# Sums of blocks turned into additions and made by adding transfers; weights asked for from ScalarE's queue

## The reference, cut to what matters

```python
h = _rmsnorm(x, norm_w)
proj = jnp.einsum('bsd,df->bsf', h, w_in)
q_a, k_a, v_a, z_a, q_m, k_m, v_m, o_m, z_m, g = jnp.split(proj, offsets, axis=-1)
# group A: QK-norm, partial rotary, three (window, dilation) patterns mixed by softmax denominators
for window, dil in ((128, 1), (512, 4), (2048, 16)):
    o, lse = _dilated_band_attention(qa, ka, va, dil, window // (2 * dil))
attn = jnp.sum(mix_w[..., None] * jnp.stack(outs, axis=0), axis=0) * jax.nn.silu(z_a)
# group B: stabilised matrix memory, chunkwise, forward and backward, summed
hm = jax.nn.sigmoid(o_m) * _rmsnorm(h_fwd + h_bwd, m_norm_w) * jax.nn.silu(z_m)
y = jnp.concatenate([attn, hm], axis=-1)
out = x + jnp.einsum('bsf,fd->bsd', y, w_out)
```

## Time and profile before

| | before |
|---|---|
| median of three runs | 1996.13 us |
| the profiled execution | 1991.36 us |
| its span | 1989.6 us |
| PE busy | 1947.4 us, 98% |
| DVE busy | 1384.3 us, 70% |
| ACT busy | 889.3 us, 45% |
| POOL busy | 222.0 us, 11% |
| granted TensorE clock, mean | 0.997 |

### The profile page before, as it was taken

One profiled execution on the slowest core, in us unless ns is written; L12 is line 12 of the kernel. 1 busy time (PEld: TensorE's weight loads), 2 busy tenths in 40 slices (PEclk: granted clock), 3 DMA queues, 4 the chain that ended last, 5 costly groups with the idle time before them and its releaser, 6 DMA issues.

```text
span 1989.6 us, 27114 instructions
## 1 busy us (share of the span) xinstructions
PE 1947.4 (98%) x9089; PEld 1589.4 (80%) x9089; DVE 1384.3 (70%) x2791; ACT 889.3 (45%) x1422; POOL 222.0 (11%) x240
## 2 busy tenths in 40 slices
PE   8999999999999999999999999999999899999999
PEld 6888887888888888888887878787787677777787
DVE  7677868678768768767767575665666857667655
ACT  6554335344335435334453335545446463455222
POOL 0241000110110010010000111110110111111111
PEclk9999999999999999999999999999999899999999
DMA  6676543564564465365369864462655836347554
GB/s 210 218 272 229 190 160 113 139 151 126 134 162 119 108 159 148 107 159 148 115 206 369 208 154 92 116 175 50 169 121 131 263 75 191 99 119 209 104 117 106
DMA packets 159337, 310.37 MB, mean 156 GB/s; under 512 B 17072, under 2 KB 36048, under 8 KB 155488
## 3 DMA queue, kind: packets, MB, share of 16 engines
q1 hardware_dynamic: 128432, 247.81, 37.8%
q0 software_dynamic: 28608, 53.49, 17.3%
q10 hardware_dynamic: 2160, 7.34, 1.0%
HBM read 198.60 MB, written 118.37 MB: 159 GB/s over the span
## 4 chain that ended last, share of the span: by engine, by line
PE 84%; DMA 5%; DVE 5%; issue 4%; ACT 1%; SPq 0%; POOL 0%; DVEq 0%; ACTq 0%; POOLq 0%
PE ps L816 22%; PE ps L820 21%; PE ps L818 21%; PE ps L1019 3%; PE ps L988 2%; PE ps L1005 2%; DMA arena<-rot_dram 1%; PE ps L957 1%; PE ps L913 1%; PE ps L922 1%; PE ps L916 1%; PE ps L1023 1%; DMA rot_dram<-arena 1%; ACT w_hi L1056 1%; PE ps L1021 1%
## 5 line engine op out<-in xcount | busy, mean ns | idle before, releaser
L816 PE MATMUL ps<-t_hi,w_hi 128*128 128x512 f32 x2184 | 872.0, 399 | 24.4 <-issue 9.7
L820 PE MATMUL ps<-t_hi,w_lo 128*128 128x512 f32 x2184 | 853.5, 391 | 0.0
L818 PE MATMUL ps<-t_lo,w_hi 128*128 128x512 f32 x2184 | 853.2, 391 | 0.0
L816 PEld LDWEIGHTS ps<-t_hi,w_hi 128*128 128x128 f32 x2184 | 411.5, 188 | 125.3 <-issue 45.9
L820 PEld LDWEIGHTS ps<-t_hi,w_lo 128*128 128x128 f32 x2184 | 411.2, 188 | 87.7
L818 PEld LDWEIGHTS ps<-t_lo,w_hi 128*128 128x128 f32 x2184 | 412.1, 189 | 79.6
L1340 DVE TENSOR_TENSOR w_lo<-s_tmp,w_hi 128x512 fp32r<-128x512 f32 x312 | 221.5, 710 | 180.0 <-ACT w_hi L1056 169.2
L1056 ACT CAST w_hi<-s_tmp 128x512 fp32r<-128x512 f32 x312 | 193.9, 622 | 292.7 <-PE ps L820 273.2
L1340 DVE TENSOR_TENSOR w_lo<-w_raw,w_hi 128x512 fp32r<-128x512 f32 x234 | 165.4, 707 | 146.9 <-ACT w_hi L1056 140.6
L1056 ACT CAST w_hi<-w_raw 128x512 fp32r<-128x512 f32 x234 | 145.4, 621 | 225.4 <-PE ps L820 225.3
L413 POOL DMA_DIRECT2D fin_dram<-xt x32 | 28.1, 878 | 850.8 <-ACT xt L1069 829.7
(11 more groups left out here) (225 smaller groups left out, 2390.5 us busy)
## 6 DMA issues: line engine op xcount, KB each, us to landing
w_raw<-w_all_dram SPq DMA_DIRECT2D x320, 256.0 KB, 4.0
fin_dram<-xt SPq DMA_DIRECT2D x128, 256.0 KB, 4.3
fin_dram<-xt POOLq DMA_DIRECT2D x128, 256.0 KB, 5.0
arena<-fin_dram SPq DMA_DIRECT2D x64, 512.0 KB, 7.3
outT_dram<-xt POOLq DMA_DIRECT2D x60, 256.0 KB, 4.1
arena<-xT_dram SPq DMA_DIRECT2D x44, 256.0 KB, 6.0
arena<-xT_dram SPq DMA_DIRECT2D x16, 512.0 KB, 4.4
outT_dram<-xT_dram SPq DMA_DIRECT2D x16, 512.0 KB, 5.4
```

The costliest lines, as they stand in the source:

```text
L816: nc.tensor.matmul(ps[:, bank, :], hi, t_hi[:, n, k, :], start=new and k == 0, stop=False, skip_group_check=True)
L818: nc.tensor.matmul(ps[:, bank, :], hi, t_lo[:, n, k, :], start=False, stop=False, skip_group_check=True)
L820: mm = nc.tensor.matmul(ps[:, bank, :], lo, t_hi[:, n, k, :], start=False, stop=k == KP - 1, skip_group_check=True)
```

## The change

Four things change, and nothing of what is computed. The signs of the operands are chosen so that every sum of blocks, of x, y and weights, is an addition (one of the four weight sums excepted); for this the evictions of n = 1 and n = 3 become `scalar_tensor_tensor` (bank times -1, minus x1). The sums of y are then made by transfers that add in DRAM: SP copies or stores the first summand, POOL adds the second. For the mLSTM half this leaves DVE altogether and is spread over units 226 to 236 and 322 to 333; for the attention half heads 4 to 6 leave DVE. The splits of the exchanges get tables of their own (`HIGH_AT`, `LOW_AT`, `Y_HIGH`, `Y_LOW`). And the weights are asked for by ACT, as the last thing of its units n = 0 and n = 4.

```diff
-Y_SPLIT = {3: {3: 0, 5: 1, 6: 2, 8: 3, 9: 4, 10: 5, 11: 6}, 4: {3: 0, 5: 1, 6: 2, 7: 3, 8: 4, 9: 5, 10: 6}}
+HIGH_AT = {1: {1: 0, 2: 1, 4: 2, 6: 3, 7: 4, 9: 6, 10: 5}, 2: {1: 0, 4: 2, 8: 6}}
+LOW_AT = {1: {1: 0, 3: 1, 5: 2, 7: 3, 8: 4, 10: 6, 11: 5}, 2: {1: 0, 5: 2, 8: 6}}
+Y_HIGH = {3: {3: 0, 4: 1, 5: 2, 7: 3, 8: 4, 9: 5, 10: 6}, 4: {3: 0, 5: 1, 6: 2, 7: 3, 8: 4, 9: 5, 10: 6}}
+Y_LOW = {3: {3: 0, 5: 1, 6: 2, 8: 3, 9: 4, 10: 5, 11: 6}, 4: {3: 0, 5: 1, 6: 2, 7: 3, 8: 4, 9: 5, 10: 6}}
-YM_AT = 321
+YM_STEPS = (226, 231, 236, 322, 328, 333)
...
@@ sync: attention_loads
-                    sp.dma_start(y_sums[:, 0, :], y_dram[ATT_HEADS + h - KP][:, HALF:]).then_inc(ya_in, 16)
-                    sp.dma_start(y_sums[:, 1, :], ty_dram[1, SUMS.index(4)][:, h - KP, :]).then_inc(ya_in, 16)
...
+                if at == 22 and h < KP:
+                    sp.dma_start(ty_dram[1, SUMS.index(3), :, h, :], ystage[:, HALF:]).then_inc(ya_out, 16)
+                    sp.wait_ge(ya_sum, h + 1)
+                    sp.dma_start(ty_dram[1, 1:4, :, h, :].rearrange("i p s -> p i s"),
+                                 y_sums[:, 0, :].unsqueeze(1).to_broadcast([P, 3, HALF])).then_inc(ya_out, 16)
+
+            def ym_copies(u):
                 y = y_dram[0:ATT_HEADS].rearrange("k p s -> p k s")
+                if u == YM_STEPS[0]:
+                    sp.wait_ge(m_out, 16 * 2)
+                    for n in (4, 3):
+                        sp.dma_start(ty_dram[0, SUMS.index(n)], y[:, 0:KP, HALF:]).then_inc(ym_out, 16)
+                if u == YM_STEPS[2]:
+                    sp.wait_ge(ym_added, 16)
+                    sp.dma_start(ty_dram[0, SUMS.index(1)], ty_dram[0, SUMS.index(4)]).then_inc(ym_out, 16)
+                if u == YM_STEPS[4]:
+                    sp.wait_ge(ym_added, 48)
+                    sp.dma_start(ty_dram[0, SUMS.index(5)], ty_dram[0, SUMS.index(1)]).then_inc(ym_out, 16)
...
@@ sync: the loop over units
-                if g + 1 < NG:
-                    next_weights(g, n)
@@ scalar: build
-                n = {1: 0, 3: 2, 4: 1, 5: 3, 6: 4, 8: 6, 9: 5}.get(off)
-                if n is not None and not (b == 2 and n in KEPT):
+                n = HIGH_AT[b].get(off)
+                if n is not None:
                     t_high(b, n)
@@ scalar
+            def next_weights(g, n):
+                if n == 0:
+                    act.wait_ge(s_done, sums_before(g) + 3)
+                    load(g + 1, 1, 0, 0)
+                    act.wait_ge(lo_done, split_before(g - 1) + 6 if g > PLAIN else 4 * PLAIN)
+                    load(g + 1, 1, 1, 1 + (g + 1) % 2)
+                    act.wait_ge(lo_done, split_before(g) + 1)
+                    load(g + 1, 0, 0, 3)
+                if n == 4:
+                    act.wait_ge(lo_done, split_before(g) + 3)
+                    act.wait_ge(s_done, sums_before(g) + 4)
+                    load(g + 1, 0, 1, 4)
...
@@ vector: evict, n == 1 (n == 3 alike)
-                    nc.vector.tensor_tensor(x2, bank, x1, ALU.add).then_inc(ev_d, 1)
+                    nc.vector.scalar_tensor_tensor(x2, bank, -1.0, x1, ALU.mult, ALU.subtract).then_inc(ev_d, 1)
@@ vector: build_sums
-                if off in (4, 5):
-                    t_four(1, 2 * off - 8)
-                    t_four(1, 2 * off - 7)
+                if off in (6, 7, 8, 9):
+                    t_four(1, off - 6)
@@ vector: ym_sums taken out, ya_sums
+                if KP <= h < ATT_HEADS - 1:
+                    return
@@ gpsimd
+            def add_ym(u):
+                y = y_dram[0:ATT_HEADS].rearrange("k p s -> p k s")
+                if u == YM_STEPS[1]:
+                    pool.wait_ge(m_out, 16 * 2)
+                    pool.wait_ge(ym_out, 32)
+                    pool.dma_start(ty_dram[0, SUMS.index(4)], y[:, 0:KP, 0:HALF], accum_op=ALU.add).then_inc(ym_added, 16)
+                if u == YM_STEPS[3]:
+                    pool.wait_ge(m_out, 16 * M_HEADS)
+                    pool.wait_ge(ym_out, 48)
+                    for n in (1, 3):
+                        pool.dma_start(ty_dram[0, SUMS.index(n)], y[:, KP:, HALF:], accum_op=ALU.add).then_inc(ym_added, 16)
+                if u == YM_STEPS[5]:
+                    pool.wait_ge(ym_out, 64)
+                    pool.dma_start(ty_dram[0, SUMS.index(5)], y[:, KP:, 0:HALF], accum_op=ALU.add).then_inc(ym_added, 16)
+
+            def add_ya(h, at):
+                if KP <= h < ATT_HEADS - 1:
+                    if at == 22:
+                        pool.wait_ge(a_y, 4 * h + 4)
+                        pool.wait_ge(ya_out, 32 * KP)
+                        pool.dma_start(ty_dram[1, 0:3, :, h - KP, :].rearrange("i p s -> p i s"),
+                                       ystage[:, HALF:].unsqueeze(1).to_broadcast([P, 3, HALF]), accum_op=ALU.add
+                                       ).then_inc(ya_added, 16)
+                    if at == 24:
+                        pool.wait_ge(ya_added, 32 * (h - KP) + 16)
+                        pool.dma_start(ty_dram[1, SUMS.index(5), :, h - KP, :], ystage[:, 0:HALF], accum_op=ALU.add
+                                       ).then_inc(ya_added, 16)
```

More of the change, by code:

```diff
@@ L1243, in y_operands @@
                     act.dma_start(t_lo[:, off - 1].bitcast(F32), y_block(3, off - 1)).then_inc(t_in[off - 1], 16)
-                n = Y_SPLIT[b].get(off)
+                n = Y_HIGH[b].get(off)
                 if n is not None:
@@ L1256, in y_operands, with load @@
                         nc.scalar.copy(t_hi[:, n, KP - 1, :], last_head(n)).then_inc(th_done[n], 1)
+            def load(g, i, k, slot):
+                p, kh = GROUPS[g]
+                act.dma_start(w_raw[:, slot, :], w_all[(2 * p + i) * PIECES + 2 * kh + k]).then_inc(w_in[slot], 16)
+            def next_weights(g, n):
[6 more added lines that the diff above has]
+                    load(g + 1, 0, 0, 3)
+                if n == 4:
+                    act.wait_ge(lo_done, split_before(g) + 3)
+                    act.wait_ge(s_done, sums_before(g) + 4)
+                    load(g + 1, 0, 1, 4)
             def plain_hi(j):
@@ L1455, in build @@
                     build_sums(off)
-                n = {1: 0, 3: 2, 4: 1, 5: 3, 6: 4, 8: 6, 9: 5}.get(off)
-                if n is not None and not (b == 2 and n in KEPT):
+                n = LOW_AT[b].get(off)
+                if n is not None:
                     t_low(b, n)
@@ L1820, in ya_sums @@
                     dve.wait_ge(a_pv, 4 * h + 4)
-                    nc.vector.tensor_tensor(y_sums[:, 0, :], high, low, ALU.subtract).then_inc(ya_sum, 1)
+                    nc.vector.tensor_tensor(y_sums[:, 0, :], high, low, ALU.add).then_inc(ya_sum, 1)
                     return
-                dve.wait_ge(ya_in, 32 * (h - KP + 1))
-                nc.vector.tensor_tensor(y_sums[:, 1, :], high, y_sums[:, 1, :], ALU.subtract).then_inc(ya_sum, 1)
-                nc.vector.tensor_tensor(y_sums[:, 0, :], high, y_sums[:, 0, :], ALU.subtract).then_inc(ya_sum, 1)
+                dve.wait_ge(ya_in, 16)
+                nc.vector.tensor_tensor(y_sums[:, 1, :], high, y_sums[:, 1, :], ALU.add).then_inc(ya_sum, 1)
+                nc.vector.tensor_tensor(y_sums[:, 0, :], high, y_sums[:, 0, :], ALU.add).then_inc(ya_sum, 1)
                 dve.wait_ge(ya_sum, sums_of_y(h) + 1)
-                nc.vector.tensor_tensor(y_sums[:, 2, :], low, y_sums[:, 1, :], ALU.subtract).then_inc(ya_sum, 1)
+                nc.vector.tensor_tensor(y_sums[:, 2, :], low, y_sums[:, 1, :], ALU.add).then_inc(ya_sum, 1)
             def y_low(b, off):
-                n = Y_SPLIT[b].get(off)
+                n = Y_LOW[b].get(off)
                 if n is not None:
```

108 lines of the change are left out of this document (32 added, 76 removed).

## The result

| | before | after |
|---|---|---|
| median of the runs, four each | 1996.99 us | 2017.18 us (2011.86 to 2018.72) |
| ratio | | 1.0095, 95% interval 1.0069 to 1.0122 |
| profiled execution | 1991.36 us | 2016.79 us, span 2015.0 |
| granted clock, mean | 0.997 | 0.992 |

A forecast was written before the change was run, and what follows sets the result against it. PE, busy 98% of the span, was taken to bound the kernel, with little idle time to touch. Terms +0.6 - 2.2 + 1.8 - 0.4 - 2.8 - 1.6 + 1.0 + 1.0 + 0.2 = -2.4 us gave 1994 us, range 1984 to 2004.

The forecast's parts named there:

- The first exchange: First exchange: PE stands 4.7 us, mostly in one gap just ahead of product 5, against 4.1 now; +0.6 us.
- The mLSTM sums: Units' idle time at 1036 to 1060 us: DVE's sums for the mLSTM half go, -2.2 us, bounds 0 and -2.2.
- The second exchange's order: Second exchange: operand 2's low part moves from `off` 3 to 5; -0.4 us, bounds 0 and -1.5.
- The third exchange's gap: Third exchange: head 4's three sums leave DVE, so PE's gap of 4.56 us shrinks to about 2.8.
- The addition at unit 333: Unit 333, among the `t_dram` loads: a 1 MB addition replaces a 1 MB load; +1.8 us, bounds 0 and +3.6.
- Stores of heads 0 to 3: Heads 0 to 3: SP stores 1 MB instead of 256 KB while turned rows travel; +1.0 us, bounds 0 and +4.
- The additions of heads 4 to 6: POOL's queue: 768 KB additions ahead of turned rows' second store and loads; +1.0 us for three heads, bounds 0 and +8.
- gains of 1.6 and 2.8: DVE's sums gone: PE's gaps behind heads 5 and 6, -1.6 us; third exchange, gap and clock together, -2.8 us.
- rival B: POOL's additions hold up turned rows of heads 5 to 7 and the `t_dram` loads: +12 us, 2008 us; chance 0.12.
- a sign of being wrong: Trace after: landings of the 768 KB additions under 4 us or over 8 us would show the forecast wrong.
- The weights from ACT: Weights asked for by ACT: nearly all in time, 0, bounds 0 and +6; `w_raw` waits over 3 us would be wrong.
- The evictions: Evictions with a scalar: 0.05 us more each, 156 times, hidden by the products except in full stretches; +0.2 us.

The follow-up runs named there:

- e8: e3 with the mLSTM half's last copy and last addition moved from units 328 and 333 to 348 and 354: 1993.5 us, 0.9972 of the kernel before.
- e3: The changed kernel with the attention half's sums made by DVE and stored by SP as before, no addition in DRAM there: 2002.3 us, 1.0026.
- e9: e3 with SP's added 768 KB of stores in heads 0 to 3 put back, in unit 22 as in the change: 2012.6 us, 1.0071.
- e7: The changed kernel, additions of heads 4 to 6 taken from y_dram, behind the turned rows' loads (units 25 and 29, not 22 and 24): 2008.0 us, 1.0047.
- e1: The changed kernel with the weights asked for by SP again, as in the kernel before: 2020.2 us, 1.0119.
- e4: The changed kernel with the mLSTM half's sums made by DVE from loaded blocks as before: 2015.5 us, 1.0090.
- e10: The changed kernel, all parts kept, the sums' DRAM transfers moved to units where the queues are nearly idle: 1992.9 us, 0.9972 of the kernel before.

## Why the prediction was wrong, by its steps

**The first exchange** came as forecast: one gap just ahead of product 5, ended by the low part on DVE,

```profile
359.15 0.47 PE L799 MATMUL ps<-t_hi,w_hi 128*128 128x512 f32 x1 [2.94 <-DVE t_lo L1453]
```

and the whole exchange neither better nor worse (excess of 300 to 380: 9.2 us before and after). PE stands 4.6 us from 324 to 370, forecast 4.7, and 4.1 before. Counting DVE's work against 11 units of products was the right way to read it.

**The mLSTM sums**, -2.2 us: the window has no gap any more. Right. **The second exchange's order**, -0.4 us, is hidden by the next step.

**The third exchange's gap**, 4.56 to 2.8 us: it is 2.79 us. Right, but a gap of 7.6 us that the forecast did not have follows it.

**The addition at unit 333**, +1.8 us with bounds 0 and +3.6: this step failed. It priced the addition by bytes over a mean rate, 6.8 us for 1 MB, and took half of the difference to what went away. The place costs 11 us (e8 against e3, 0.54%, with the copy ahead of it). An addition of 1 MB took 14.5 us with no large transfer beside it and 19.7 us here; PE waits here for the landing of each load, one product at a time, the loads land 6 to 7 us later, and PE then loses clock too. The row with `t_dram` already at 1.0 us of wait said that there was no slack.

**Stores of heads 0 to 3**, +1.0 us with bounds 0 and +4: this step failed too, with 9 us measured (e9 against e3). The bytes, 0.13% or 2.6 us, lie within the bounds. The other 6 us are a step that the prediction did not have: SP's wait for DVE's sum, moved from unit 23 to 22, holds back the next head's first load, so that 768 KB, both loads of `rs_dram` and the second store of turned rows fall together.

**The additions of heads 4 to 6**, +1.0 us with bounds 0 and +8, against gains of 1.6 and 2.8, so -3.4 us together: in their place they cost 0.24%, 5 us (after against e9, the two intervals overlap), and in units 25 and 29 they give as much (e7 against e9). The mechanism was rival B's, priced at 12 us with a chance of 0.12, and the rows for it were there: a store and a load within 0.6 us in one queue, a wait of DVE for them. The forecast set it aside because "DVE has slack before PE stands". At the third exchange DVE had none. The prediction charged heads 5 to 7 and did not look at which exchange head 5's turned rows fall in. The 768 KB were priced at 5.0 us; they landed in 9.5, 11.2 and 18.1 us, over the 8 us that it had named as a sign of being wrong. Even so rival B falls short of the measured time by 9 us: its sum had the last addition at 3.6 us and the stores of heads 0 to 3 not at all.

**The weights from ACT**, 0 with bounds 0 and +6: four pairs lie between -0.25% and +0.19%, 5 us to either side, so no constant cost, but no constant zero either. The waits of DVE and ACT for `w_raw` beside the kernel's first grow to 3.4 + 1.8 + 0.4 = 5.6 us, over the 3 us named as a sign; with the weights on SP (e1) 3.7 us of such waits stay and the time is no better. **The evictions**, +0.2 us for 0.05 us more each: the two forms take the same time at this shape (L1358 and L1361 685 ns, L1354 and L1357 691 and 690 ns as the median of 78), so there was nothing to charge.

Along the chain of kernels from before to after, the sum is -0.28% for the rest of the change (e8), +0.54% for the late copy and addition (e3), +0.45% for the stores (e9) and +0.24% for the additions of heads 4 to 6. These are differences of neighbours, so they add up to the 0.95% whatever they hold; each has an error of 0.2 to 0.3%, and taking a part out of the changed kernel instead gives other sizes (0.48% for the additions in e7, 0.05% for the whole mLSTM half in e4). Against the forecast's terms the first two steps are 9 and 8 us too small, and the third, 5 us of cost for 3.4 us of gain, is 8 us off.

## What to carry to other kernels

A transfer is priced by what lands beside it and what stands behind it in its queue and behind its wait in its engine's program, not by its bytes over a mean rate: the same parts of a change made this kernel 20 us slower or 6 us faster (e10), by the unit in which their transfers were asked for. When work is taken off a busy engine and put into DRAM, look first for the stretches with a low DMA share, and put it there, behind the small transfers for which an engine is waiting. Where a trace shows even 1 us of wait for a load, that load has no slack left, and what is put beside it must be priced by what it does to the landing. And one pair of kernels is not enough for a gain of a few us: here the same part gave 9 us on one base and nothing on another.
